# Where a tile's own queries and routes lie among its experts: a first quarter against a first half

## The reference

```python
    def block(xi):                                   # 128 rows
        qv = (xi @ wq).reshape(B, PEER_BLOCK, PEER_HEADS, 2, half)
        s = jnp.einsum('bthpc,hpnc->bthpn', qv, sub_keys).astype(jnp.float32)
        top_s, top_i = lax.top_k(s, K)               # K = 16
        ...
        best_s, best_j = lax.top_k(cand_s, K)
        expert = jnp.take_along_axis(cand_i, best_j, axis=-1)
        gate = jax.nn.softmax(best_s, axis=-1)
        act = jax.nn.gelu(jnp.einsum('btd,bthkd->bthk', xi, u_tab[expert]).astype(jnp.float32), approximate=False)
        return jnp.einsum('bthk,bthkd->btd', (gate * act).astype(xi.dtype), v_tab[expert])
```

## Time and profile before

| | before |
|---|---|
| median of 3 runs | 2979.73 us |
| lowest and highest | 2973.87 and 2981.59 us |
| the profiled execution | 2973.29 us, span 2971.5 us |
| PE busy | 2618.1 us (88%) |
| DVE busy | 1431.6 us (48%) |
| ACT busy | 916.0 us (31%) |
| POOL busy | 681.0 us (23%) |
| moved by DMA | 839.09 MB, mean 282 GB/s |

### The profile page before, as it was taken

One profiled execution on the slowest core, in us unless ns is written; L12 is line 12 of the kernel. 1 busy time (PEld: TensorE's weight loads), 2 busy tenths in 40 slices (PEclk: granted clock), 3 DMA queues, 4 the chain that ended last, 5 costly groups with the idle time before them and its releaser, 6 DMA issues.

```text
span 2971.5 us, 30335 instructions
## 1 busy us (share of the span) xinstructions
PE 2618.1 (88%) x11408; PEld 1774.3 (60%) x11408; DVE 1431.6 (48%) x3191; ACT 916.0 (31%) x2318; POOL 681.0 (23%) x615
## 2 busy tenths in 40 slices
PE   7776999878999995999998899999799999878776
PEld 6665888755884884766554566565376655443222
DVE  3776333242001234665546654545665554676444
ACT  1452111220000120354523235432334442333333
POOL 0010111110000001223233323333322333433432
PEclk9888999998999997999999999999899999999999
DMA  6220211214332665998999898999999899998997
GB/s 253 85 78 38 77 66 43 71 57 156 142 142 107 262 242 213 395 394 359 365 418 419 347 389 356 421 411 419 388 359 400 337 383 416 408 378 332 419 421 329
DMA packets 109986, 839.09 MB, mean 282 GB/s; under 512 B 12176, under 2 KB 12432, under 8 KB 13968
## 3 DMA queue, kind: packets, MB, share of 16 engines
q0 software_dynamic: 73728, 536.90, 44.8%
q1 hardware_dynamic: 36112, 300.25, 25.6%
HBM read 836.06 MB, written 1.05 MB: 282 GB/s over the span
## 4 chain that ended last, share of the span: by engine, by line
PE 61%; DVE 15%; DMA 14%; ACT 7%; issue 2%; POOL 1%; SPq 0%; POOLq 0%; DVEq 0%; ACTq 0%
PE psm L2129 17%; DMA mem<-in_puv,mem 14%; PE psm L427 10%; PE psm L1701 6%; PE psm L435 5%; DVE mem L2173 3%; PE psm L1348 3%; PE psm L716 3%; PE psm L2004 3%; PE psm L1245 3%; PE psm L1891 2%; PE psm L1396 1%; DVE mem L672 1%; PE psm L431 1%; PE psm L731 1%
## 5 line engine op out<-in xcount | busy, mean ns | idle before, releaser
L2129 PE MATMUL psm<-mem 128*128 128x512 f32 x2048 | 1017.5, 625 | 164.7 <-ACT mem L2147 160.8
L2173 DVE CUSTOM_DVE_ANT_0 mem<-mem 128x1024 f32<-128x1024 f32 x512 | 624.4, 1223 | 466.8 <-DMA mem<-in_puv,mem 463.0
L2157 POOL DMA_INDIRECT mem<-in_puv,mem x512 | 563.4, 1100 | 1205.4 <-PE psm L2129 1146.0
L2129 PEld LDWEIGHTS psm<-mem 128*128 128x128 f32 x2048 | 376.0, 196 | 607.8 <-ACT mem L2147 300.5
L427 PE MATMUL psm<-mem 128*128 128x256 f32 (+2 forms) x1504 | 355.1, 400 | 55.7 <-DVE mem L534 36.0
L427 PEld LDWEIGHTS psm<-mem 128*128 128x128 f32 x1504 | 294.5, 198 | 115.5 <-issue 52.7
L2141 ACT ACTIVATE mem<-mem 128x1 f32<-128x1 f32 x512 | 102.3, 200 | 692.0 <-DVE mem L2173 688.9
L1701 PE MATMUL psm<-mem 128*128 128x256 f32 x1024 | 243.7, 385 | 0.5 <-ACT mem L1424 0.5
L1701 PEld LDWEIGHTS psm<-mem 128*128 128x128 f32 x1024 | 196.2, 193 | 68.8 <-issue 45.0
L2147 ACT ACTIVATE mem<-mem 128x128 f32<-128x128 f32 x512 | 206.0, 402 | 17.0 <-PE psm L2129 0.3
L435 PE MATMUL psm<-mem 128*128 128x128 f32 x1408 | 191.2, 280 | 19.4 <-ACT mem L984 5.9
(11 more groups left out here) (356 smaller groups left out, 2413.6 us busy)
## 6 DMA issues: line engine op xcount, KB each, us to landing
mem<-in_w2g SPq DMA_DIRECT2D x64, 1024.0 KB
mem<-in_w SPq DMA_DIRECT2D x18, 2048.0 KB, 8.4
mem<-in_pwq SPq DMA_DIRECT2D x32, 1024.0 KB
mem<-in_w2f SPq DMA_DIRECT2D x28, 1024.0 KB
mem<-in_wgu SPq DMA_DIRECT2D x11, 2048.0 KB, 7.5
mem<-in_w2t SPq DMA_DIRECT2D x20, 1024.0 KB
mem<-in_w2b SPq DMA_DIRECT2D x16, 1024.0 KB
mem<-in_w2o SPq DMA_DIRECT2D x16, 1024.0 KB
```

Of the source, the lines that this page charges most:

```text
L2129: m = pe.matmul(bank(6 + h), DG[:, n % 4, :], GR[n % PING][:, 1024 + h * 512:1536 + h * 512], start=k == 0, stop=k == 127)
L2157: po.indirect_dma_start(GR[n % PING], None, A[f"puv{i // 2}"], bass.IndirectOffsetOnAxis(ap=IX[i % 2][:, k:k + 1], axis=0)).then_inc(gsem[ ...
L2173: ve.tensor_tensor_reduce(out=GR[n % PING][:, 0:1024], in0=GR[n % PING][:, 0:1024], in1=X[:, i % 2, :], scale=1.0, scalar=0.0, op0=MUL, op ...
```

## The change

The own steps no longer have a spread of their own. In tiles 0 to 2 they are merged evenly (`merged`) with that part of the next tile's lane that stands ahead of its first nsa step (fm, tm, the first core steps, one of gates), and the whole lane is laid over 114 experts from position 7.5 (1.5 in tile 0). By the weights the merged part takes 52 experts. In the last tile, which prepares no other, the own steps are spread over 75 experts from 7.5. The finish of the tile before gets fixed positions, 1.5 + 0.6 n. No instruction is added or left out, and every wait stays; the order of loads follows the plan.

```diff
@@ -256,20 +256,26 @@
             front = ["fm"] * 28 + ["ht1"] * (i == 0) + ["tm"] * 4 + weave([("tm", 10, 1), ("core", 7, 0.7)])
             return front + weave([("gates", 32, 1), ("nsa", 22, 1), ("core", 14, 0.7)]) + ["mix"] * 24 + ["query"] * 8 + ["route"] * 20
 
+        def merged(a, b):
+
+            at_ = [((n + 0.5) / len(a), s) for n, s in enumerate(a)] + [((n + 0.5) / max(len(b), 1), s) for n, s in enumerate(b)]
+            return [s for _, s in sorted(at_, key=lambda x: x[0])]
+
         plan = [(s, 0) for s in tile_steps(0)]
         for i in RI:
-            placed_at = [(128.0 * i + k, ("e", 128 * i + k)) for k in range(128)]
-            lane = [("fin", i - 1)] * 10 * (i >= 1) + [(s, i + 1) for s in (tile_steps(i + 1) if i < 3 else [])]
-            total, done = sum(weight[s] for s, _ in lane), 0.0
+            own = []
+            for c in R3:
+                own += [("query", i)] * 8 + [("route", i)] * 20
+            lane = [(s, i + 1) for s in (tile_steps(i + 1) if i < 3 else [])]
+            until = lane.index(("nsa", i + 1)) if i < 3 else 0
+            lane = merged(own, lane[:until]) + lane[until:]
+            total, done, span = sum(weight[s] for s, _ in lane), 0.0, 114.0 if i < 3 else 75.0
+            spread = [(128.0 * i + k, ("e", 128 * i + k)) for k in range(128)]
+            spread += [(128.0 * i + 1.5 + 0.6 * n, ("fin", i - 1)) for n in range(10 * (i >= 1))]
             for s in lane:
-                placed_at.append((128.0 * i + 1.5 + 118 * done / total if i < 3 else 128.0 * i + 1.5 + done, s))
+                spread.append((128.0 * i + (7.5 if i else 1.5) + span * done / total, s))
                 done += weight[s[0]]
-            lane = []
-            for c in R3:
-                lane += [("query", i)] * 8 + [("route", i)] * 20
-            for n, s in enumerate(lane):
-                placed_at.append((128.0 * i + 0.2 + 33.0 * n / len(lane), s))
-            plan += [s for _, s in sorted(placed_at, key=lambda x: x[0])]
+            plan += [s for _, s in sorted(spread, key=lambda x: x[0])]
         plan += [("e", NE), ("e", NE + 1)] + [("fin", 3)] * 10
 
 
```

## The result

The changed kernel took 3000.38 us (median of five runs, 2994.34 to 3003.51), the kernel before 2974.83 us beside it (2972.71 to 2981.59). The ratio is 1.0086, with a 95% interval of 1.0072 to 1.0099: slower by 0.9%, where 2940 and a range up to 2982 had been forecast. The profiled span is 2998.6 us against 2971.5, 27.1 us longer.

The account below looks back on a forecast made before the run. DMA bytes were taken to bound the expert stretch, with only losses against 422 GB/s to win. Gains of 8 + 8 + 10 + (17 - 3) = 40 us gave 2940 us from the median 2979.7, range 2916 to 2982.

Parts of the forecast that it names:

- The last tile: Last tile: spreading the own steps shortens DVE's waits for scores; about 17 us gained, less 3 for late indices.
- late indices: Last tile: POOL waits for chunk 1's indices at expert 32's gather; 2.6 us once, between 0 and 7.
- Experts 0 to 8: Start of a tile: PE's 6.64 us wait for the finish shortens, winning 2 of 5.5 us.
- Experts 8 to 60: Tiles 1 and 2: PE per expert falls below DMA, so the 10.1 us loss goes, 2 us left.
- The block: Keys' compression, a block of tiny matmuls in each earlier tile: loses its 11.4 us as before.
- Experts 60 to 128: Denser gates and nsa, experts 60 to 98: 16 us lost against 13.6 before, bounds 11 and 45.
- mix: Denser mix steps after the gates, 13.5 experts: no loss taken, up to 5 us.
- by their losses: Tiles 0 and 2, not cut into pieces: gains of 8 and 10 us taken from losses of 35.6 and 41.8.
- own sign of being wrong: Stretch of the gates: forecast wrong if it runs under 380 GB/s beyond the block, or granted clock falls there.
- (c): Rival, dense stretch of the earlier tiles: lower granted clock makes it slower, 17 us a tile, 2991 us; chance 0.11.
- (a): Rival: earlier tiles keep their losses as PE binds at 60 to 98, only the last tile gains; 2966 us, chance 0.16.
- (b): Rival: earlier tiles keep their losses, last tile's spread routes hold DVE, late indices cost 7 us; 2980 us, chance 0.11.

Follow-up runs that it names:

- e9: e1 with the own steps of tiles 0 to 2 over 39 experts instead of 33 (35.5 in tile 0); 2962.82 us.
- e7: The changed kernel with the own steps of tiles 0 to 2 over 33 experts as before, the next tile's steps unmoved; 3004.46 us.
- e13: The changed kernel with tiles 0 to 2's merged part over experts 7.5 to 39.6 (tile 0: 1.5 to 36), the rest where before had it; 2969.75 us.
- e14: The changed kernel with half of the gates' matmuls and half of their weights' bytes left out; 2944.18 us.
- e16: e1 with half of the gates' matmuls and half of their weights' bytes left out; 2895.15 us.
- e4: The changed kernel with the last 20 route steps of the preparation in tiles 0 to 2 laid 0.36 instead of 0.27 experts apart; 2996.14 us.
- e8: The changed kernel with every second matmul of the gates left out, loads and waits kept; 2971.91 us.
- e3: The changed kernel with the merged part packed into experts 7.5 to 45 and the rest spread over 45 to 121.5 (tile 0 ends differ); 2979.98 us.
- e1: The kernel before with only the last tile following the new plan, tiles 0 to 2 as before; 2957.09 us.
- e11: e1 with five gather buffers instead of six; 3039.65 us.
- e10: The changed kernel with five gather buffers instead of six; 3089.66 us.

## Why the prediction was wrong

**The last tile was right, in size and in mechanism.** Forecast 14 us gained, measured 15.3. Its first three pieces, after:

```profile
2649.00:2696.00 47.00, 39.12 (x136) 21.07 (x135) 25.45 (x42) 15.10 (x50) 18.80 (x18) 0.89 0.96 389
2696.00:2744.00 48.00, 34.30 (x64) 11.57 (x63) 33.04 (x98) 17.57 (x52) 16.58 (x16) 0.93 0.95 391
2744.00:2786.00 42.00, 38.02 (x138) 19.87 (x137) 25.65 (x69) 15.47 (x50) 18.21 (x16) 1.00 1.01 420
```

DVE no longer holds 42.31 of 60 and 42.56 of 52 us but 25.45 of 47 and 33.04 of 48, and the loss of these pieces fell from 23.9 to 7.5 us (7 were left over in the sum). From the first dot product to that of expert 33 it is 98.6 us instead of 114.4 (the forecast had 98 instead of 112; 112.1 is the time to expert 32, which is now 95.1). No wait of DVE for the scores (20.9 us in the earlier trace rows, there L2047 on L2036, here L2053 on L2042) is among DVE's waits in 2649 to 2749 any more. The late indices came as priced. POOL's timeline after:

```profile
2728.70 0.95 POOL L2163 DMA_INDIRECT mem<-in_puv,mem  x1 [1.30 <-PE psm L2135]
2738.20 0.95 POOL L2163 DMA_INDIRECT mem<-in_puv,mem  x1 [8.54 <-DVE mem L2113]
```

and DVE's timeline, its dot products 31, 32 and 33:

```profile
2739.03 1.23 DVE L2179 CUSTOM_DVE_ANT_0 mem<-mem 128x1024 f32<-128x1024 f32 x1 [0.32 <-DMA mem<-in_puv,mem]
...
2743.82 1.23 DVE L2179 CUSTOM_DVE_ANT_0 mem<-mem 128x1024 f32<-128x1024 f32 x1 [3.45 <-DMA mem<-in_puv,mem]
2747.35 1.23 DVE L2179 CUSTOM_DVE_ANT_0 mem<-mem 128x1024 f32<-128x1024 f32 x1 [2.30 <-DMA mem<-in_puv,mem]
```

POOL waits 8.54 us for L2113 (the L2107 of the earlier trace rows), the gather issued at 2738.20 is used at 2743.82, 5.62 us later (5.75 assumed), and the gap from 31 to 32 is 4.79 us, 2.3 over the period of 2.49 (2.6 forecast). By the fit of the Trainium skill ("DMA: Bandwidth & Descriptors", Anatomy of one DMA) an estimate is 4.4 us. The measured 5.62 lies nearer to the row of before, though it holds the releases between POOL, DMA and DVE too.

**Experts 0 to 8: right.** PE's wait of 6.64 us for the finish is 1.17 for the same op, L2208 before and L2214 now, though 5.08 stand ahead of it at an earlier op of the finish (2.19 before), together 6.3 instead of 8.8 us. The first eight experts of tile 1 lose 3.1 us instead of 6.3 (forecast were 2 less). PE's timeline:

```profile
1674.92 11.03 PE L2135 MATMUL psm<-mem 128*128 128x512 f32 x20 [5.08 <-DVE mem L2194]
1687.12 1.09 PE L437 MATMUL psm<-mem 128*128 128x128 f32 x8 [1.17 <-DVE mem L2214]
```

**Experts 8 to 60: the first step that failed.** "So PE falls below DMA, and the 10.1 us loss goes ... I leave 2 us": with the 2 us of experts 0 to 8 this was 10 us a tile. Ahead of the block tile 1 went from 15.7 to 12.0 us of loss, a gain of 3.7, tile 2 from 13.0 to 13.9 and tile 0 from 7.6 to 13.8. So over three tiles 3.4 us were lost where tile 1's 10 us, taken three times, would be 30 gained, and tile 1, the only one that the prediction cut into pieces, was the one that gained. Its first piece was to be at 400 GB/s and reached 380, and the second, which had lost nothing, now loses 5.2 with PE busy 54.32 of 60 us. The step compared totals of PE and DMA. It left out what the prediction counts for the last tile: each own chunk starts with a wait of DVE for its scores. Before, these three waits of tile 1 were 7.0, 12.8 and 3.4 us long, in its first 26 experts; after they are 3.7, 7.5 and 5.1, at experts 13, 28 and 47, the 7.5 in the second piece. In tile 0 they were 7.1, 6.0 and 6.5 and are 6.2, 7.7 and 5.3: moved, not gone. e9 shows the same trade: own steps laid wider move loss from the first piece to the second.

**The block: right.** It lost 11.5 us before and 11.8 after, at a clock of 0.87 over its piece; over three tiles 43.2 and 42.2.

**Experts 60 to 128: the step that turned the sign.** "Outside it PE 3.5 and DMA 3.5 us are even. I take 5 us for that, 16 against 13.6 before". In tile 1 the three pieces from expert 48 lose 11.8 + 1.1 + 9.6 = 22.5 us: over the 16, within the bounds of 11 and 45. For mix "I take 0, up to 5", and its piece, the seventh, loses 0.1: right. The tail, chunk 0 of the next tile behind mix, is as dense as the rest and has no term in the sum; it loses 10.7 us instead of 4.2. In tiles 0 and 2, "by their losses" taken to gain 8 and 10 us, the pieces behind the block lose 11.7 and 16.1 us more than before, in tile 1 14.6. That makes 42.4 us in three tiles; tile 1's term of 2.4, taken three times, is 7. The prediction's own sign of being wrong, under 380 GB/s beyond the block, is there: 353 in the sixth piece. The step compared the total of PE with the total of DMA, found both to fit, and left the time at which each piece of work waits for another engine unpriced. DVE's waits in the sixth piece, after (total us, times, longest):

```profile
DVE mem L1854 <- PE psm L1778: 9.9, 2, 7.1
DVE mem L1839 <- ACT mem L1795: 5.5, 2, 4.6
DVE mem L2179 <- DMA mem<-in_puv,mem: 4.9, 5, 1.6
```

DVE stands 15.4 of 58 us waiting at two lines of nsa, three times as long as for gathers. It takes its work in order, so the next dot product stands behind. PE in turn waits 8.2 us in this piece, all for the experts' activations (L2135 for L2153) and none for a load of weights. Before, the same lines stood in the piece from 1908 to 1959, which lost 2.1 us:

```profile
DVE mem L1833 <- ACT mem L1789: 5.0, 2, 3.9
DVE mem L1848 <- PE psm L1772: 1.9, 1, 1.9
```

With all other waits for something that isn't a gather, DVE stood 17.6 of 51 us there and stands 22.8 of 58 after. In the same pieces of tiles 0 and 2 it stood 24.5 and 20.7 us, with losses of 10.0 and 6.4, and stands 25.8 and 27.9, with 7.8 and 14.1: more waiting, more loss, but for tile 0. The tail shows the whole circle, first in DVE's timeline:

```profile
2134.94 0.19 DVE L2112 SCALAR_TENSOR_TENSOR mem<-mem 128x32 uint32<-128x32 f32 x1
2135.05 0.18 DVE L2113 TENSOR_TENSOR mem<-mem 128x32 f32<-128x32 f32 x1
...
2138.21 1.22 DVE L2179 CUSTOM_DVE_ANT_0 mem<-mem 128x1024 f32<-128x1024 f32 x1
...
2139.36 1.22 DVE L2179 CUSTOM_DVE_ANT_0 mem<-mem 128x1024 f32<-128x1024 f32 x1
...
2140.50 1.22 DVE L2179 CUSTOM_DVE_ANT_0 mem<-mem 128x1024 f32<-128x1024 f32 x1
...
2147.37 1.23 DVE L2179 CUSTOM_DVE_ANT_0 mem<-mem 128x1024 f32<-128x1024 f32 x1 [5.64 <-DMA mem<-in_puv,mem]
```

then PE's and POOL's timelines and the stretch from 2137 to 2144:

```profile
2137.82 8.66 PE L2135 MATMUL psm<-mem 128*128 128x512 f32 x13 [6.15 <-ACT mem L2153]
```

```profile
2131.94 1.26 POOL L2163 DMA_INDIRECT mem<-in_puv,mem  x1 [1.29 <-PE psm L2135]
2141.88 0.95 POOL L2163 DMA_INDIRECT mem<-in_puv,mem  x1 [8.68 <-PE psm L2135]
```

```profile
2137.00:2144.00 7.00, 6.18 (x8) 2.71 (x9) 4.73 (x11) 4.46 (x17) 0.95 (x1) 0.53 0.10 20
```

Until 2136 DVE is at the route steps of the next tile's chunk 0. Then the dot products of the gathers that had long landed follow 1.15 us apart, with no wait for DMA. A buffer comes free only when PE has used it as well (L2135), and PE had stood 6.15 us for them; so POOL issues nothing for 8.68 us and DMA moves 20 GB/s for 7 us. DVE then waits 5.64 us for the first new gather. Before, chunk 0's route steps stood there too, 0.36 instead of 0.27 experts apart, with a dot product between more of them; PE's longest wait was 5.0 us and POOL's 7.4, and the piece lost 4.2 us. In tiles 0 and 2 the tail went from 3.5 and 1.8 to 8.3 and 9.8 us. In the sixth piece the same is milder: in stretches of 2 us the lowest rate there is about 210 GB/s, not 20.

What of this is shown: e7 and e13 show the place, the density behind the own steps. e14 against e16 shows that the load of the gates isn't what parts the plans. The traces show the circle of waits, in full in the tail, and e4, which lays the tail's route steps as far apart as before, takes 1.8 to 3.4 us a tile off its loss. That the waits make up the whole 42 us is argued by exclusion and not shown. Their sum alone doesn't settle it: DVE's waits for something other than a gather are 280 us in tiles 0 to 2 before, 353 after and 282 in e8, whose tiles are as long as those of after; and the seventh piece of tile 1 holds 29.8 us of them and loses 0.1. Which wait of the second half costs most stays open. e3 has 9.4 of tile 1's 20.3 us in the two late pieces left, with the second half 1.23 times thinner (76.5 experts for what after lays over 62.0).

**The rivals.** (c), the only one on this side, put the slowdown in this stretch but gave it to a lower granted clock, at a mean below 0.92. Pieces five and seven stand at 1.00 and 0.99, the sixth at 0.94, and it fell where PE was idle, 49.75 of 58 us busy; that PE ran slower there is a companion and hardly the cause, since halving PE's matmuls of the gates (e8) left the tiles' lengths as they were at a clock of 0.93. No run holds the clock and changes the plan. (a) and (b) supposed that the earlier tiles keep their losses, and they lost more. What should have been a rival is "DVE in order, at 1.29 times the density": the earlier trace rows shows such waits, 20.9 us in three, where the prediction used them for the last tile, and it stopped there.

**Open.** e3 lays its second half at 2.07 units an expert, close to the 1.99 of before, and is still 23 us above e1. By the losses it is 24.1 us, of which 16.7 lie in the last four pieces, so density alone may not be the whole account: at 1.99 (e13) the same pieces lose 4.3 us more than in e1. Why five buffers cost e1, which has little of the dense stretch, as much as the changed kernel isn't settled.

## What to carry to other kernels

When steps of several engines are laid into one order, the sums of work per engine say whether a stretch can fit, not whether it does; count for each step the wait that the in-order engine has to stand through before it may serve the saturated stream, and ask how close such waits come together. Comparing one wait with what the buffers hold isn't enough: here that is five further gathers, 12 us, the longest wait of DVE in the sixth piece was 7.1 us, and yet 9.6 us were lost. A stretch that runs hidden at one density need not at 1.29 times that, even with PE and DMA both below their limits. A gain that is read in one tile isn't a gain in its siblings: cut each of them. And where a change acts on stages one by one, run each half alone: here one half was worth 18 us, and the other cost 42.

## What the hardware showed beyond the question

- One gather buffer less, five instead of six, cost 83 and 89 us of some 1800 us of expert work, in all tiles (e11 against e1, e10 against after). By period alone, five gathers of 2.49 us are 12.4 us of cover, against 5.62 us from the issue of a lone gather to its use.
- Less work on PE brought no higher clock: with half of the gates' matmuls gone, the mean granted clock was 0.934 instead of 0.944 (e8), and e14's sixth piece stood at 0.88 against 0.94. Right after PE's wait of 6.15 us the clock was 0.53, with PE busy 6.18 of 7 us. The Trainium skill ("TensorE: Matmul & The Clock Gate", Part 1) says that the throttled state is the default and activity releases it. These rows agree with that. The block of tiny matmuls doesn't plainly: there 0.68 was granted with PE busy throughout.
